# The experts' down projection in a mixture-of-experts block, taken in plain fp32 instead of high and low halves

## Chip, core and metric

The kernel runs on one core of a Trainium2 chip. The metric is the time of the whole program on the device in microseconds, the median of several runs. TensorE (PE) multiplies, VectorE (DVE) and ScalarE (ACT) work elementwise, GpSimd (POOL) works elementwise too and issues the indexed DMAs, SyncE (SP) issues the weight loads.

## What is computed

The model is a diffusion transformer of two layers on 512 latent and 256 context tokens of width 1024, all in fp32. Each layer has an attention and then a mixture of 64 experts, of which every token takes 8. The part of the reference that matters here, cut to its core:

```python
def routed_experts(xf, top_idx, top_w, w_gate, w_up, w_down):
    ...
    def body(acc, blk):
        tok, w, e = blk
        xb = x_pad[tok]
        h = jax.nn.silu(xb @ w_gate[e]) * (xb @ w_up[e])
        return acc.at[tok].add((h @ w_down[e]) * w[:, None]), None
    ...
```

A block is up to 128 tokens of one expert; xb is 128 x 1024, h is 128 x 256. The weights of one expert are 3 MB in fp32.

## The kernel before

The program is a row of stages with a barrier between them: modulation, projections, attention, output projection, routing, experts, combination, and the same again for the second layer. The change is in `stage_experts(l, nt, moe)`, which runs once per layer. Each engine has its own program there; they meet by semaphores.

All engines walk through the same steps (`all_steps`): a loop over pairs of experts, so that the buffer index j (0 or 1) is a constant, and inside it a loop over the blocks of an expert whose bounds are read from `starts_i`. Most experts have one block; where one has more, the further ones are steps without change of expert. `step(b, j, change, e, split)` is the step of block b; with `change`, block b is the first of expert e+1, and `split` says that the weights of expert e+2 are split in this step.

To reach near fp32 precision with the fast fp32r operands, every factor is kept as a high half (a copy rounded to fp32r) and a low half (the original minus the high half), and `product` forms three products for each pair: high with high, high with low, low with high. The halves:

- gate and up weights: raw in `gu_raw`, ScalarE writes `gu_hi` (L1524), VectorE `gu_lo` (L1590).
- down weights: raw in `d_raw`, ScalarE writes `d_hi` (L1530), GpSimd `d_lo` (L1404, `split_down`).
- the rows of the block, gathered into `xb` (L1395), are turned on TensorE into `psX` (L1457), and split into `xT_hi` (L1514) and `xT_lo` (L1582).
- the hidden rows `hh` (L1585: silu(gate) times up) are turned into `psH` (L1467), and split into `hT_hi` (L1553, ScalarE) and `hT_lo` (L1606, VectorE).

TensorE's order in one step is: turn the hidden rows of block b-1; the gate and up product of block b, 24 products of 512 columns into `psG`; turn the gathered rows of block b+1; the down product of block b-1, 12 products of 512 columns into `psY`. ScalarE's order: `hT_hi`, the two high halves of gate and up, silu, `xT_hi`, the left half of `yb` out of `psY`, the high half of down. VectorE's: `hT_lo`, the two low halves of gate and up, the gating product, `xT_lo`, the right half of `yb`. GpSimd's: wait for the scatter of the step before, copy its index (`si`), gather the rows of block b+2, scatter block b-1 (a DMA that adds into `acc_d`), then the low half of down.

SyncE loads the raw weights in six parts of 512 KB per expert, in the order gate, gate, up, up, down, down, with at most three parts in flight (AWAY = 3). Each raw buffer has room for two experts, and so have the halves. A raw buffer is loaded anew when its split is done: before part 0 SyncE waits for the low half of gate, before part 2 for that of up, and before part 4 for that of down:

```python
elif m == 4:
    sp.wait_ge(s_dl, e + 1)
```

The waits of the down product are:

```python
def down_of(b, j, e):
    pe.wait_ge(s_hTl, b + 1)
    pe.wait_ge(s_dl, e + 1)
    pe.wait_ge(s_ya, b + 1)
    pe.wait_ge(s_yd, b + 1)
    down(j)
```

Of the kernel before, what the change touches and what calls it, by code (L numbers as in the profile page):

```python
# [6 lines left out]
F32 = mybir.dt.float32  # L7
# [3 lines left out]
F32R = mybir.dt.float32r  # L11
ALU = mybir.AluOpType
# [3 lines left out]
P = 128  # L16
D = 1024
# [90 lines left out]
def build(nc, a, out):  # L108
    with ExitStack() as whole:
# [1192 lines left out]
        def stage_experts(l, nt, moe):  # L1302
# [6 lines left out]
            with ExitStack() as ctx:  # L1309
# [6 lines left out]
                d_hi = T("d_hi", [P, 2, KF, D], F32R)  # L1316
                d_lo = T("d_lo", [P, 2, KF, D], F32R)
# [5 lines left out]
                hT_hi = T("hT_hi", [P, KF, P], F32R)  # L1323
                hT_lo = T("hT_lo", [P, KF, P], F32R)
# [9 lines left out]
                s_guh, s_gul, s_dh, s_dl = S("guh"), S("gul"), S("dh"), S("dl")  # L1334
                s_tx, s_gu, s_ht, s_dn = S("tx"), S("gu"), S("ht"), S("dn")
                s_xh, s_xl, s_sil, s_mul, s_hTh, s_hTl, s_ya, s_yd = (S(n) for n in ("xh", "xl", "sil", "mul", "hTh", "hTl", "ya", "yd"))
# [26 lines left out]
                with nc.Block() as block:  # L1363
                    @block.sync
                    def _(sp):
                        with sp.Fori(0, NE // 2 - 1) as i:
                            for j in range(2):
                                e = 2 * i + j
                                for m in range(PARTS):

                                    if m == 0:
                                        sp.wait_ge(s_gul, 2 * e + 1)
                                    elif m == 2:
                                        sp.wait_ge(s_gul, 2 * e + 2)
                                    elif m == 4:
                                        sp.wait_ge(s_dl, e + 1)
                                    sp.sem_inc(s_bear, 1)


                                    sp.wait_ge(s_raw[m % AWAY], raw_loads(e + 2, m) - 16)  # L1380
                                    sp.sem_inc(s_bear, 1)
                                    load_part(sp, l, moe, j, e + 2, m)

                    @block.gpsimd
                    def _(pool):
# [16 lines left out]
                        def split_down(j, e):  # L1402
                            pool.wait_ge(s_dh, e + 1)
                            G.tensor_tensor(d_lo[:, j], d_raw[:, j], d_hi[:, j].bitcast(F32), ALU.subtract).then_inc(s_dl, 1)  # L1404

# [18 lines left out]
                        split_down(0, 0)  # L1424
# [4 lines left out]
                        split_down(1, 1)  # L1429

                        def step(b, j, change, e, split):
                            take_rows(b - 1)
                            pool.wait_ge(s_tx, b + 2)
                            gather(b + 2)
                            give(b - 1)
                            if split:
                                split_down(j, e + 2)
# [11 lines left out]
                    def _(pe):  # L1449
# [20 lines left out]
                        def down(j):  # L1470
                            for n in range(2):
                                c = slice(n * 512, (n + 1) * 512)
                                product(nc, psY[:, n], [(hT_hi[:, k], hT_lo[:, k], d_hi[:, j, k, c], d_lo[:, j, k, c]) for k in range(KF)], s_dn if n == 1 else None)
# [9 lines left out]
                        def down_of(b, j, e):  # L1483
                            pe.wait_ge(s_hTl, b + 1)
                            pe.wait_ge(s_dl, e + 1)
                            pe.wait_ge(s_ya, b + 1)
                            pe.wait_ge(s_yd, b + 1)
                            down(j)

                        def step(b, j, change, e, split):  # L1490
# [8 lines left out]
                            down_of(b - 1, j, e)  # L1499

                        def last(b):
                            pe.wait_ge(s_mul, b)
                            turn_hidden()
                            down_of(b - 1, 1, NE - 1)
# [6 lines left out]
                    def _(act):  # L1511
# [14 lines left out]
                        def split_down(j, e, loading=True):  # L1526
                            if loading:
                                for m in (4, 5):
                                    act.wait_ge(s_raw[m % AWAY], raw_loads(e, m))
                            nc.scalar.activation(d_hi[:, j], d_raw[:, j], ACT.Copy).then_inc(s_dh, 1)  # L1530


# [3 lines left out]
                        split_down(0, 0, False)  # L1536
# [3 lines left out]
                        split_down(1, 1, False)  # L1540
# [10 lines left out]
                        def hidden(b):  # L1551
                            act.wait_ge(s_ht, b + 1)
                            nc.scalar.activation(hT_hi[:], psH[:, 0:KF], ACT.Copy).then_inc(s_hTh, 1)  # L1553

                        def step(b, j, change, e, split):
# [9 lines left out]
                            if split:  # L1565
                                split_down(j, e + 2)
# [8 lines left out]
                    def _(dve):  # L1575
# [28 lines left out]
                        def hidden(b):  # L1604
                            dve.wait_ge(s_hTh, b + 1)
                            V.tensor_tensor(hT_lo[:], psH[:, 0:KF], hT_hi[:].bitcast(F32), ALU.subtract).then_inc(s_hTl, 1)  # L1606

                        def step(b, j, change, e, split):
                            hidden(b - 1)
# [7 lines left out]
                        def last(b):  # L1617
                            hidden(b - 1)
                            out_of(b - 1)
# [513 lines left out]
```

## Time and profile before

| | |
|---|---|
| median of 3 runs | 3462.98 us (3459.09 to 3465.24) |
| span of the profiled execution | 3452.0 us |
| PE busy | 2794.7 us (81%) |
| DVE busy | 2159.4 us (63%) |
| ACT busy | 1509.0 us (44%) |
| POOL busy | 1260.6 us (37%) |
| DMA | 643.04 MB, mean 186 GB/s |
| splits of down weights | x128 on ACT and x128 on POOL |
| blocks of both layers | 144 |

The profiled execution spans 3452.0 us from its first to its last instruction; the times of the runs also hold what lies around it, some 11 us. The two stages of the experts run from about 838 to 1830 us and from about 2490 to 3415 us. Busy times are sums over the whole program, so they do not tell which wait ends last in a stage.

### The profile page before, as it was taken

Reading aid. Unit: us, or ns where it says so; the run is one execution under the profiler, and the core shown is the slowest. Engines: PE = TensorE matmul, PEld = TensorE weight load, DVE = VectorE, ACT = ScalarE, POOL = GpSimd, SP = SyncE. Lnnn points to the kernel's source line nnn. Section 1 sums busy time; section 2 is a strip of 40 time slices with the busy share of each in tenths; the row PEclk is TensorE's granted clock in tenths of the full one; section 3 lists DMA queues with packets and bytes.
Section 4 is the critical chain, followed back from the end, with each engine's and each line's share of the span. In section 5 each row is a group of like instructions: output and inputs, shape, how many; then the busy total and the mean of one; then the engine's idle time right before and its main releaser. Section 6 shows DMA issues by size and latency. Waiting matters only on the chain. (4 is left out here: it accounts for less than half of the span.)

```text
span 3452.0 us, 46471 instructions
## 1 busy us (share of the span) xinstructions
PE 2794.7 (81%) x12826; PEld 2105.5 (61%) x12827; DVE 2159.4 (63%) x2406; ACT 1509.0 (44%) x2033; POOL 1260.6 (37%) x856
## 2 busy tenths in 40 slices
PE   8899999877888888778882788867788877888884
PEld 2266677754666676566661677756476656666663
DVE  7733345436666657878764465543667878778884
ACT  5521334312555545555552233322255655555552
POOL 1000000111555546555564000002165655556554
PEclk9999999988989999999995999988899999998997
DMA  9820100232898888999982111002489999889994
GB/s 357 316 74 5 37 1 1 71 135 107 252 275 268 252 228 260 294 289 291 287 236 88 56 38 37 19 5 113 186 245 280 273 287 285 267 270 271 278 286 133
DMA packets 206943, 643.04 MB, mean 186 GB/s; under 512 B 30664, under 2 KB 41928, under 8 KB 206336
## 3 DMA queue, kind: packets, MB, share of 16 engines
q1 hardware_dynamic: 162464, 518.83, 42.9%
q0 software_dynamic: 43232, 118.78, 16.5%
q10 hardware_dynamic: 1152, 4.19, 0.3%
q8 instruction: 57, 0.93, 0.1%
q14 instruction: 38, 0.31, 0.0%
HBM read 587.06 MB, written 90.28 MB: 196 GB/s over the span
## 5 line engine op out<-in xcount | busy, mean ns | idle before, releaser
L1590 DVE TENSOR_TENSOR F_gu_lo<-gu_raw,F_gu_hi 128x2048 fp32r<-128x2048 f32 x256 | 996.6, 3932 | 178.4 <-ACT F_gu_hi L1524 177.0
L1404 POOL TENSOR_TENSOR F_d_lo<-d_raw,F_d_hi 128x2048 fp32r<-128x2048 f32 x128 | 657.6, 5138 | 0.0
L101 PE MATMUL F_psG<-F_gu_hi,F_xT_hi 128*128 128x512 f32 x1152 | 506.7, 440 | 76.6 <-DVE F_xT_lo L1582 74.0
L102 PE MATMUL F_psG<-F_gu_lo,F_xT_hi 128*128 128x512 f32 x1152 | 488.4, 424 | 0.0
L103 PE MATMUL F_psG<-F_gu_hi,F_xT_lo 128*128 128x512 f32 x1152 | 487.6, 423 | 0.0
L1524 ACT ACTIVATE F_gu_hi<-gu_raw 128x2048 fp32r<-128x2048 f32 x256 | 475.6, 1913 | 13.3 <-PEq L126 13.3
L101 PEld LDWEIGHTS F_psG<-F_gu_hi,F_xT_hi 128*128 128x128 f32 x1152 | 241.4, 210 | 147.1 <-issue 78.6
L1457 PE MATMUL F_psX<-cst,F_xb 128*128 128x128 f32 x1168 | 173.3, 295 | 146.6 <-DMA F_xb<-f_d,F_gi 146.2
L1409 POOL COPY F_si<-tok 128x1 int32 x144 | 83.2, 578 | 552.1 <-DMA acc_d<-F_yb,F_si 552.0
L1399 POOL DMA_INDIRECT acc_d<-F_yb,F_si x146 | 232.5, 1592 | 118.5 <-issue 93.0
L103 PEld LDWEIGHTS F_psG<-F_gu_hi,F_xT_lo 128*128 128x128 f32 x1152 | 240.0, 208 | 56.8
L1549 ACT ACTIVATE F_yb<-F_psY,wgt 128x512 f32<-128x512 f32 x144 | 99.1, 688 | 399.3 <-POOL F_si L1409 299.3
L102 PEld LDWEIGHTS F_psG<-F_gu_lo,F_xT_hi 128*128 128x128 f32 x1152 | 241.6, 210 | 49.7
L1457 PEld LDWEIGHTS F_psX<-cst,F_xb 128*128 128x128 f32 x1168 | 151.9, 194 | 190.2 <-DMA F_xb<-f_d,F_gi 186.2
L1514 ACT ACTIVATE F_xT_hi<-F_psX 128x512 fp32r<-128x512 f32 x292 | 158.8, 596 | 220.0 <-PE F_psX L1457 220.0
L101 PE MATMUL F_psY<-F_d_hi,F_hT_hi 128*128 128x512 f32 x576 | 250.5, 435 | 4.6 <-DVE F_hT_lo L1606 4.6
L1530 ACT ACTIVATE F_d_hi<-d_raw 128x2048 fp32r<-128x2048 f32 x128 | 243.7, 1904 | 0.0
L103 PE MATMUL F_psY<-F_d_hi,F_hT_lo 128*128 128x512 f32 x576 | 237.9, 413 | 0.0
L102 PE MATMUL F_psY<-F_d_lo,F_hT_hi 128*128 128x512 f32 x576 | 236.8, 411 | 0.0
L1582 DVE TENSOR_TENSOR F_xT_lo<-F_psX,F_xT_hi 128x512 fp32r<-128x512 f32 x292 | 186.7, 679 | 41.8 <-ACT F_xT_hi L1514 41.8
L1395 POOL DMA_INDIRECT F_xb<-f_d,F_gi x148 | 161.2, 1089 | 128.6 <-ACT F_yb L1549 71.3
L954 POOL TENSOR_TENSOR h<-h,D_y 128x1024 f32<-128x1024 f32 x10 | 23.6, 2360 | 413.3 <-DVE D_y L937 413.3
(306 smaller groups left out, 4903.5 us busy)
## 6 DMA issues: line engine op xcount, KB each, us to landing
gu_raw<-in_we_gate_dram SPq DMA_DIRECT2D x256, 512.0 KB
gu_raw<-in_we_up_dram SPq DMA_DIRECT2D x256, 512.0 KB
d_raw<-in_we_down_dram SPq DMA_DIRECT2D x256, 512.0 KB
wada<-in_w_ada_dram SPq DMA_DIRECT2D x24, 2048.0 KB, 11.0
I_w_raw<-in_wc_in_dram SPq DMA_DIRECT2D x32, 384.0 KB, 5.8
acc_d<-o SPq DMA_DIRECT2D x12, 512.0 KB, 2.6
f_d<-D_f SPq DMA_DIRECT2D x10, 512.0 KB, 2.6
H_ac<-acc_d SPq DMA_DIRECT2D x10, 512.0 KB, 8.9
```

The costliest lines, as they stand in the source:

```text
L101: nc.tensor.matmul(acc, xh, wh, start=(start and i == 0), stop=False)
L102: nc.tensor.matmul(acc, xh, wl, start=False, stop=False)
L103: ins = nc.tensor.matmul(acc, xl, wh, start=False, stop=(stop and i == n - 1))
L1395: pool.indirect_dma_start(xb[:], None, f_d[l][0:nt * P], bass.IndirectOffsetOnAxis(ap=gi[:].bitcast(U32), axis=0), bounds_check=nt * P - 1 ...
L1399: pool.indirect_dma_start(acc_d[l], bass.IndirectOffsetOnAxis(ap=si[:].bitcast(U32), axis=0), yb[:], None, compute_op=ALU.add).then_inc(s_ ...
L1404: G.tensor_tensor(d_lo[:, j], d_raw[:, j], d_hi[:, j].bitcast(F32), ALU.subtract).then_inc(s_dl, 1)
L1457: ins = nc.tensor.transpose(psX[:, k // 4, k % 4], v[:, k], ident)
L1514: nc.scalar.activation(xT_hi[:, 4 * n:4 * n + 4], psX[:, n], ACT.Copy).then_inc(s_xh, 1)
L1524: nc.scalar.activation(gu_hi[:, j, v], gu_raw[:, j, v], ACT.Copy).then_inc(s_guh, 1)
L1530: nc.scalar.activation(d_hi[:, j], d_raw[:, j], ACT.Copy).then_inc(s_dh, 1)
L1582: V.tensor_tensor(xT_lo[:, k], psX[:, n], xT_hi[:, k].bitcast(F32), ALU.subtract).then_inc(s_xl, 1)
L1590: V.tensor_tensor(gu_lo[:, j, v], gu_raw[:, j, v], gu_hi[:, j, v].bitcast(F32), ALU.subtract).then_inc(s_gul, 1)
```

## The change

The down product takes `d_raw` itself and one `hT`, both plain fp32. The high and low halves of the down weights and of the turned hidden rows are gone, and so are the tiles that held them. Four matmul calls of 512 columns stand where twelve stood. Because TensorE now reads the raw buffer, SyncE's wait before part 4 is for a new semaphore, `s_last`, which TensorE raises after the last down product of an expert has ended; TensorE waits for its own product there. The down product now waits for the loads of the parts 4 and 5.

```diff
-                d_hi = T("d_hi", [P, 2, KF, D], F32R)
-                d_lo = T("d_lo", [P, 2, KF, D], F32R)
...
-                hT_hi = T("hT_hi", [P, KF, P], F32R)
-                hT_lo = T("hT_lo", [P, KF, P], F32R)
+                hT = T("hT", [P, KF, P])
...
                                     elif m == 4:
-                                        sp.wait_ge(s_dl, e + 1)
+                                        sp.wait_ge(s_last, e + 1)
                                     sp.sem_inc(s_bear, 1)
...
-                        def split_down(j, e):
-                            pool.wait_ge(s_dh, e + 1)
-                            G.tensor_tensor(d_lo[:, j], d_raw[:, j], d_hi[:, j].bitcast(F32), ALU.subtract).then_inc(s_dl, 1)
...
                         def down(j):
                             for n in range(2):
                                 c = slice(n * 512, (n + 1) * 512)
-                                product(nc, psY[:, n], [(hT_hi[:, k], hT_lo[:, k], d_hi[:, j, k, c], d_lo[:, j, k, c]) for k in range(KF)], s_dn if n == 1 else None)
+                                for k in range(KF):
+                                    ins = nc.tensor.matmul(psY[:, n], hT[:, k], d_raw[:, j, k, c], start=(k == 0), stop=(k == KF - 1))
+                            ins.then_inc(s_dn, 1)
...
-                        def down_of(b, j, e):
-                            pe.wait_ge(s_hTl, b + 1)
-                            pe.wait_ge(s_dl, e + 1)
+                        def down_of(b, j, e, change):
+                            pe.wait_ge(s_hT, b + 1)
+                            for m in (4, 5):
+                                pe.wait_ge(s_raw[m % AWAY], raw_loads(e, m))
                             pe.wait_ge(s_ya, b + 1)
                             pe.wait_ge(s_yd, b + 1)
                             down(j)
+                            if change:
+                                pe.wait_ge(s_dn, b + 1)
+                                pe.sem_inc(s_last, 1)
...
-                            nc.scalar.activation(d_hi[:, j], d_raw[:, j], ACT.Copy).then_inc(s_dh, 1)
...
-                            nc.scalar.activation(hT_hi[:], psH[:, 0:KF], ACT.Copy).then_inc(s_hTh, 1)
+                            nc.scalar.activation(hT[:], psH[:, 0:KF], ACT.Copy).then_inc(s_hT, 1)
...
-                            V.tensor_tensor(hT_lo[:], psH[:, 0:KF], hT_hi[:].bitcast(F32), ALU.subtract).then_inc(s_hTl, 1)
```

GpSimd in a step with a change of expert, before: index copies, gather (`F_xb`), scatter (`acc_d`), then the split of down.

```order
L1409 COPY F_si<-tok 128x1
L1433 REGISTER_ALU
L1392 ISA
L1392 COPY F_gi<-tok 128x1
L1393 REGISTER_ALU
L1395 DMA F_xb<-f_d,F_gi 128x1024
L1412 REGISTER_ALU
L1399 DMA acc_d<-F_yb,F_si 896x1024
L1403 REGISTER_ALU
L1404 TENSOR_TENSOR F_d_lo<-d_raw,F_d_hi 128x2048
L1347 TENSOR_LOAD starts_i
```

The same step after the change.

```order
L1402 COPY F_si<-tok 128x1
L1424 REGISTER_ALU
L1389 ISA
L1389 COPY F_gi<-tok 128x1
L1390 REGISTER_ALU
L1392 DMA F_xb<-f_d,F_gi 128x1024
L1405 REGISTER_ALU
L1396 DMA acc_d<-F_yb,F_si 896x1024
L1344 TENSOR_LOAD starts_i
```

The split `F_d_lo` behind the scatter is gone; the rest keeps its order. ScalarE in the same step, before, from the turned hidden rows to the end.

```order
L1553 ACTIVATE F_hT_hi<-F_psH 128x256
L1523 ISA
L1524 ACTIVATE F_gu_hi<-gu_raw 128x2048
L1523 REGISTER_ALU
L1524 ACTIVATE F_gu_hi<-gu_raw 128x2048
L1560 REGISTER_ALU
L1517 ACTIVATE F_sil<-F_psG 128x256
L1562 REGISTER_ALU
L1514 ACTIVATE F_xT_hi<-F_psX 128x512 x2
L1549 ISA
L1549 ACTIVATE F_yb<-F_psY,wgt 128x512
L1530 ACTIVATE F_d_hi<-d_raw 128x2048
```

And after.

```order
L1539 ACTIVATE F_hT<-F_psH 128x256
L1518 ISA
L1519 ACTIVATE F_gu_hi<-gu_raw 128x2048
L1518 REGISTER_ALU
L1519 ACTIVATE F_gu_hi<-gu_raw 128x2048
L1546 REGISTER_ALU
L1512 ACTIVATE F_sil<-F_psG 128x256
L1548 REGISTER_ALU
L1509 ACTIVATE F_xT_hi<-F_psX 128x512 x2
L1535 ISA
L1535 ACTIVATE F_yb<-F_psY,wgt 128x512
```

`F_d_hi` at the end is gone, and the two high halves of gate and up stand, as before, ahead of the silu, the turned rows and the output.

## Rows read from the trace of the kernel before

**Rows 1.** The page's head.

```profile
span 3452.0 us, 46471 instructions
```

**Rows 2.** Table by stretch: PE, PEld, DVE, ACT, POOL busy us; clock, DMA share, GB/s.

```profile
2700.00:3000.00 300.00, 241.05 (x1012) 187.37 (x1013) 238.25 (x155) 168.53 (x174) 174.10 (x109) 0.92 0.92 282
```

**Rows 3.** List of waits from 2500 to 3400: us in total, times, longest.

```profile
POOL F_si L1409 <- DMA acc_d<-F_yb,F_si: 257.6, 66, 6.4
```

**Rows 4.** Timeline of GpSimd in one step: start us, duration, work [idle before].

```profile
2837.29 0.74 POOL L1409 COPY F_si<-tok 128x1 int32 x1 [3.66 <-DMA acc_d<-F_yb,F_si]
...
2840.99 1.60 POOL L1399 DMA_INDIRECT acc_d<-F_yb,F_si  x1 [0.90 <-issue]
2842.03 5.18 POOL L1404 TENSOR_TENSOR F_d_lo<-d_raw,F_d_hi 128x2048 fp32r<-128x2048 f32 x1
2850.60 1.02 POOL L1409 COPY F_si<-tok 128x1 int32 x1 [3.38 <-DMA acc_d<-F_yb,F_si]
```

**Rows 5.** Timeline of GpSimd: a step without split; ends of a 25-step run.

```profile
1120.67 1.59 POOL L1399 DMA_INDIRECT acc_d<-F_yb,F_si  x1 [0.30 <-issue]
1127.06 0.18 POOL L1409 COPY F_si<-tok 128x1 int32 x1 [4.80 <-DMA acc_d<-F_yb,F_si]
...
1397.06 0.19 POOL L1409 COPY F_si<-tok 128x1 int32 x1 [4.21 <-DMA acc_d<-F_yb,F_si]
...
1741.58 0.18 POOL L1409 COPY F_si<-tok 128x1 int32 x1 [3.90 <-DMA acc_d<-F_yb,F_si]
```

**Rows 6.** List of waits of SyncE's queue, 2500 to 3400.

```profile
SPq L1377 <- POOL F_d_lo L1404: 245.4, 61, 6.8
```

**Rows 7.** Timeline of SyncE's queue: issues of weight parts, in pairs.

```profile
2840.54 2.83 SPq L1023 DMA_DIRECT2D gu_raw<-in_we_up_dram  x2
2847.44 0.92 SPq L1023 DMA_DIRECT2D d_raw<-in_we_down_dram  x2
2850.87 2.21 SPq L1023 DMA_DIRECT2D gu_raw<-in_we_gate_dram  x2
```

**Rows 8.** The page's groups: work, count | busy us, mean ns | idle before, releaser.

```profile
L1404 POOL TENSOR_TENSOR F_d_lo<-d_raw,F_d_hi 128x2048 fp32r<-128x2048 f32 x128 | 657.6, 5138 | 0.0
L1524 ACT ACTIVATE F_gu_hi<-gu_raw 128x2048 fp32r<-128x2048 f32 x256 | 475.6, 1913 | 13.3 <-PEq L126 13.3
L1409 POOL COPY F_si<-tok 128x1 int32 x144 | 83.2, 578 | 552.1 <-DMA acc_d<-F_yb,F_si 552.0
```

**Rows 9.** One line of VectorE: count, min/median/max ns, first and last start.

```profile
L1590 DVE TENSOR_TENSOR F_gu_lo<-gu_raw,F_gu_hi x256: 2276/2290/8040, 841.7 to 3387.3; 128x2048 fp32r<-128x2048 f32 x128
```

**Rows 10.** Timeline of VectorE: the gating product.

```profile
2851.50 0.41 DVE L1585 TENSOR_TENSOR F_hh<-F_sil,F_psG 128x256 f32<-128x256 f32 x1
```

**Rows 11.** Timeline of TensorE: gate_up starts, down's first and last, hidden turned, gate_up.

```profile
2839.65 0.49 PE L101 MATMUL F_psG<-F_gu_hi,F_xT_hi 128*128 128x512 f32 x1 [0.77 <-DVE F_xT_lo L1582]
...
2846.06 0.48 PE L101 MATMUL F_psY<-F_d_hi,F_hT_hi 128*128 128x512 f32 x1
...
2848.67 0.39 PE L103 MATMUL F_psY<-F_d_hi,F_hT_lo 128*128 128x512 f32 x1
2851.96 0.68 PE L1467 MATMUL F_psH<-cst,F_hh 128*128 128x128 f32 x2 [2.91 <-DVE F_hh L1585]
2853.24 0.79 PE L101 MATMUL F_psG<-F_gu_hi,F_xT_hi 128*128 128x512 f32 x1 [0.60 <-issue]
```

**Rows 12.** Timeline of TensorE: a plain fp32 down product of the shared expert.

```profile
2446.53 3.70 PE L1139 MATMUL E_psY<-E_wd,E_hT 128*128 128x512 f32 x8 [0.80 <-ACT E_hT L1195]
```

**Rows 13.** The page's DMA queues: packets, MB, share of 16 engines' span.

```profile
q1 hardware_dynamic: 162464, 518.83, 42.9%
q0 software_dynamic: 43232, 118.78, 16.5%
```

**Rows 14.** The page's DMA issues: count, size of each, median us to landing.

```profile
f_d<-D_f SPq DMA_DIRECT2D x10, 512.0 KB, 2.6
```

## What the change was predicted to do

> **What bounds the kernel now.** The change touches only the stage of the experts, so I looked at the two long stretches of that stage first. The table by stretch [rows 2] shows DMA at 0.92 of its 16 engines, TensorE busy 80% (241.05 of 300 us), VectorE 79%, and a granted clock of 0.92: no engine is full, only DMA is near it. The list of waits [rows 3] says what the rhythm hangs on: GpSimd waits 257.6 us, 66 times, of the second stage for the scatter of the step before. The GpSimd timeline [rows 4] shows the loop: copy of the index at 2837.29, scatter issued at 2840.99, landed 9.6 us later at 2850.60. 3.7 us of issue and 9.6 us of landing make a step of 13.3 us. Over a long run of steps the copy starts at 1397.06 and 25 steps later at 1741.58 [rows 5], so a steady step takes 344.5 / 25 = 13.78 us. Where a block belongs to the same expert as the one before, so that no weights are split, the scatter issued at 1120.67 has landed at 1127.06 [rows 5]: 6.4 us. The landing is long where weight loads run beside it.
>
> Second, the weight loads. SyncE waits 245.4 us, 61 times, for the split of the down weights on GpSimd [rows 6]; at 2847.44 the loads start 0.3 us after that split ends (2842.03 + 5.13 = 2847.16) [rows 4, 7]. So the stream of loads runs as far ahead as its buffers allow: a raw buffer is free as soon as the split of the weights is done, two steps before they are multiplied.
>
> **What is removed, and its worth.** Per expert: on ScalarE the high half of the down weights (128x2048 like a gate or up half, 1.91 us [rows 8]), on GpSimd the low half, 5.14 us [rows 8], per block a small low half on VectorE. GpSimd's 5.14 us lie inside the 9.6 us in which it would wait for the scatter anyway [rows 4], so without it GpSimd only waits longer: worth nothing directly. But it slows VectorE: the low halves of gate and up take 2.29 us in the median and up to 8.04 us [rows 9]. After the change I count them at 2.29 us. The Trainium skill, page SBUF — State Buffer, section "SBUF: two separate sides", says that the port pair that GpSimd and a VectorE operation with two inputs in SBUF share is an exclusive lock, so the loser waits for the whole operation; 2.29 + 5.14 = 7.4 us would be such a case, and by that rule the change is a gain for VectorE.
>
> **What is dearer: the product itself.** Now 12 products of 512 columns; the last of them starts 2848.67 - 2846.06 = 2.61 us after the first and takes 0.39: 3.0 us [rows 11]. The same product in plain fp32 (two stationary tiles, two halves of 512 columns) stands in the trace before, in the shared expert: 8 records in 3.70 us [rows 12]. So +0.7 us at full clock, and at 1.2 GHz up to twice that; I take +0.8. Where TensorE is not what ends the step this is covered by its waits, such as 2.91 us before the turn of the hidden rows [rows 11].
>
> **What is moved: the release of the buffers.** This is the term that decides. The down weights of expert x+2 can now be loaded only when down(x) has read its buffer, at the end of its step; before, it was when they had been split, two steps earlier. On SyncE's queue the four gate and up parts of expert x+3 stand behind these two. They have to be split on ScalarE in the very next step and multiplied in the one after. The queue of prefetch falls from over one step ahead to nothing, and a loop closes over two steps:
> end of down(x), six parts landed (L), second half copied on ScalarE 1.91, its low half 2.29 [rows 8, 9], from the start of the gating product to the start of gate_up 2853.24 - 2851.50 = 1.74, from the start of gate_up over the turned rows to the start of down 2846.06 - 2839.65 = 6.41 [rows 10, 11], down 3.70 [rows 12], issue on SyncE 0.33 (the second of a pair ends its issue so much after its start; an estimate from the 0.92 us of a pair [rows 7]). Without L this is 16.4 us.
> L comes from the queues [rows 13]: the hardware queue moved 518.83 MB in 42.9% of 3452 us, 2.85 us per MB, so the 3.15 MB of an expert need 8.98 us; the software queue needs 16.5% of 3452 / 118.78 = 4.8 us per MB, the scatter (0.52 MB) 2.5 us. A transfer of 512 KB alone lands 2.6 us after its issue [rows 14], 1.1 more than its 1.5 us of work. With half of the scatter inside the burst L is 11.3, with all of it 12.6. The scatter of down(x) starts with the burst, so I take 12.1. Bounds: no sharing at all, 10.1; and by the parts of now, where the second of the pair issued at 2840.54 was out by 2843.04 and let the next go at 2850.87 [rows 7], 7.8 us with three in flight, 2.6 each, 15.6 for six.
> The clock: at 0.92 granted [rows 2], some 0.16 of the time is at 1.2 GHz, half of whose work is lost: 0.08 x 13.8 = 1.1 us a step. That lies in TensorE's waits now and on the path then, with one pass of TensorE per two steps: +1.1.
> Step after: (12.1 + 16.4 + 1.1) / 2 = 14.8 us. At the bounds of L without and with the clock: 13.3 (then the scatter's 13.78 holds) and 16.6. GpSimd's own loop, 3.7 + some 11 if the scatter shares the whole burst, is about as long, so it gives no relief. In return, the gather falls into the lull behind the burst; its wait on TensorE is hidden by then.
>
> **The sum.** There are 144 blocks, 128 of them with a new expert [rows 8]; 16 are repeats. A repeat and the step behind it have their loads early, and each stage has about four steps of run-in and run-out; that leaves 144 - 32 - 8 = 104 steady steps and 40 others. Steady: 104 x (14.8 - 13.78) = +106. Others: bound by TensorE, 40 x 0.8 = +32. At the start of both stages the first splits of down go, some 2 us of ScalarE each: -4. Sum +134 on a span of 3452.0 [rows 1]: 3586. The median of the runs, 3463, is 11 us above the span, so 3597, rounded to 3600.
>
> **The rivals.**
> (a) The loads keep up (L near its lower bound, 13.3 < 13.78), the scatter sets the step as now. Then only the other steps pay: +28, 3490. For it: DMA has some 7% of lull now; against: the sum above 12 us.
> (b) Faster. GpSimd is free and VectorE's two low halves take 4.6 us, where one alone now takes up to 8.04 [rows 9]; in the step shown the gating product comes at 2851.50 and TensorE has waited 2.91 us for it [rows 10, 11]. It decides if L stays under 10.5 and if the scatter, which today meets loads in any phase, then lands against fewer of them: with 0.8 us less landing a step, 104 x -0.8 + 28 = -55, 3408. For it: the scatter that lands in 6.4 us [rows 5]. Against: the burst starts with the scatter.
> (c) Much slower. TensorE's single long wait per step lets the clock fall in most steps; with 4 us instead of 1.1 and L at 13, the step is 16.7, +304 + 28, 3795.
> (d) Gains and losses cancel within 7 us, 3463.
>
> **How the numbers follow.** Chances: the forecast 0.62, (a) 0.13, (b) 0.12, (c) 0.08, (d) 0.05. Predicted is the forecast's 3600. The range takes in (a) and (d) and steps up to 15.8 us in the forecast: 3458 to 3710; (b) and (c) are left out. A measurement of this kernel can tell about 0.2%, 7 us, from no change. Faster 0.12, within 0.2% 0.06, slower 0.82.
>
> **What would show it.** In the trace after, the list of SyncE's waits should be led by the product of down, the pair of down loads should be issued within a microsecond of its end and the gate loads right behind, ScalarE should wait for DMA before the high halves of gate and up (it does nowhere now), and TensorE longer before the turn of the hidden rows; VectorE's low halves should be at 2.3 us. A burst shorter than 10.5 us, or ScalarE not waiting for loads, would prove the forecast wrong; so would a scatter that lands in 8 us.

## The result and the profile after

The changed kernel takes 3861.18 us (3844.42 to 3863.99, 4 runs) against 3461.03 us before, a ratio of 1.1139 with an interval of 1.1112 to 1.1166: 11.4% slower, 400 us. The forecast was 3600 us, range 3458 to 3710. The direction and the mechanism held, the size did not: the loss is 400 us where some 140 were forecast.

The head and some groups of the page after, to be set beside [rows 1, 8, 9]. The columns are work, count | busy, mean ns | idle before, releaser.

```profile
span 3862.3 us, 44917 instructions
...
PE 2986.9 (77%) x12250; PEld 2071.3 (54%) x12251; DVE 1687.9 (44%) x2262; ACT 1290.6 (33%) x1905; POOL 636.4 (16%) x728
...
L1574 DVE TENSOR_TENSOR F_gu_lo<-gu_raw,F_gu_hi 128x2048 fp32r<-128x2048 f32 x256 | 585.0, 2292 | 1153.6 <-ACT F_gu_hi L1519 1153.2
L1519 ACT ACTIVATE F_gu_hi<-gu_raw 128x2048 fp32r<-128x2048 f32 x256 | 487.2, 1913 | 910.4 <-DMA gu_raw<-in_we_gate_dram 666.7
```

VectorE, ScalarE and GpSimd work less than before, TensorE more, and VectorE's low halves are at 2.29 us in the mean, 2364 ns at most, as forecast; and everything ends later. ScalarE, which waited for no load before [rows 8], is now idle for 910.4 us before its high halves, 666.7 us of it until a load of the gate weights lands. The waits of SyncE's queue over the whole program (us, times, longest), beside [rows 6]:

```profile
SPq L1374 <- PEq L1483: 1127.5, 123, 27.5
```

L1483 is TensorE's signal that down has ended. The loads wait for it once per expert, up to 27.5 us. By stretch, from 3000 to 3300, beside [rows 2]:

```profile
3000.00:3300.00 300.00, 220.34 (x755) 150.67 (x756) 118.19 (x106) 105.64 (x121) 58.08 (x71) 0.82 0.76 227
```

The DMA share fell from 0.92 to 0.76 and the granted clock from 0.92 to 0.82. How a step goes is told by the timelines of the same 35 us (start us, duration, work [idle before, releaser]). TensorE:

```profile
3113.05 3.60 PE L1463 MATMUL F_psY<-d_raw,F_hT 128*128 128x512 f32 x8
...
3126.99 3.60 PE L1463 MATMUL F_psY<-d_raw,F_hT 128*128 128x512 f32 x8
...
3136.28 0.70 PE L1456 MATMUL F_psH<-cst,F_hh 128*128 128x128 f32 x2 [5.70 <-DVE F_hh L1569]
3137.56 0.79 PE L101 MATMUL F_psG<-F_gu_hi,F_xT_hi 128*128 128x512 f32 x1 [0.58 <-DVE F_xT_lo L1566]
3138.14 0.63 PE L102 MATMUL F_psG<-F_gu_lo,F_xT_hi 128*128 128x512 f32 x1
3138.57 0.63 PE L103 MATMUL F_psG<-F_gu_hi,F_xT_lo 128*128 128x512 f32 x1
...
3143.26 0.53 PE L102 MATMUL F_psG<-F_gu_lo,F_xT_hi 128*128 128x512 f32 x1
3143.63 0.39 PE L103 MATMUL F_psG<-F_gu_hi,F_xT_lo 128*128 128x512 f32 x1
3143.86 0.40 PE L101 MATMUL F_psG<-F_gu_hi,F_xT_hi 128*128 128x512 f32 x1
...
3146.81 3.60 PE L1463 MATMUL F_psY<-d_raw,F_hT 128*128 128x512 f32 x8
```

SyncE's issues and ScalarE's high halves:

```profile
3116.97 0.90 SPq L1023 DMA_DIRECT2D d_raw<-in_we_down_dram  x2
3118.37 3.20 SPq L1023 DMA_DIRECT2D gu_raw<-in_we_gate_dram  x2
3123.13 2.66 SPq L1023 DMA_DIRECT2D gu_raw<-in_we_up_dram  x2
```

```profile
3129.21 1.91 ACT L1519 ACTIVATE F_gu_hi<-gu_raw 128x2048 fp32r<-128x2048 f32 x1 [9.62 <-DMA gu_raw<-in_we_gate_dram]
3131.66 1.91 ACT L1519 ACTIVATE F_gu_hi<-gu_raw 128x2048 fp32r<-128x2048 f32 x1 [0.54 <-DMA gu_raw<-in_we_up_dram]
```

VectorE and GpSimd:

```profile
3133.60 2.29 DVE L1574 TENSOR_TENSOR F_gu_lo<-gu_raw,F_gu_hi 128x2048 fp32r<-128x2048 f32 x1 [0.16 <-ACT F_gu_hi L1519]
3135.81 0.41 DVE L1569 TENSOR_TENSOR F_hh<-F_sil,F_psG 128x256 f32<-128x256 f32 x1
```

```profile
3115.09 1.05 POOL L1392 DMA_INDIRECT F_xb<-f_d,F_gi  x1 [0.87 <-POOL F_gi L1389]
3118.36 1.59 POOL L1396 DMA_INDIRECT acc_d<-F_yb,F_si  x1 [2.21 <-DVE F_yb L1586]
3128.64 0.19 POOL L1402 COPY F_si<-tok 128x1 int32 x1 [8.69 <-DMA acc_d<-F_yb,F_si]
```

Follow one turn of the loop. Down ends at 3113.05 + 3.60 = 3116.65. 0.3 us later the six parts begin to go out. The last part of up is there at 3131.66, 15.0 us after the end of down. Then come the high half (1.94 us until the low half starts), the low half (2.21 until the gating product at 3135.81), the turned hidden rows (1.75 until gate_up starts at 3137.56), and the next down but one at 3146.81, ended at 3150.41. 15.01 + 1.94 + 2.21 + 1.75 + 9.25 + 3.60 = 33.76 us for two steps. Between them lies a short step (3116.65 to 3130.59), which runs on loads that came in time, and a long one of 19.8 us. From the down product at 3044.69 to the one 14 steps later at 3283.45 a step takes 17.05 us, where it took 13.78 [rows 5]. Below, L is the time from the end of down to the start of the high half of the last up part.

### The profile page after: what moved, and what is told of

It reads as the page before. It is cut to its first block and busy times, and to the rows that moved or that the text cites. A ratio compares the mean times of both kernels' runs of the same rounds, so it can differ in the third digit from the quotient of the medians.

```text
span 3862.3 us, 44917 instructions
## 1 busy us (share of the span) xinstructions
PE 2986.9 (77%) x12250; PEld 2071.3 (54%) x12251; DVE 1687.9 (44%) x2262; ACT 1290.6 (33%) x1905; POOL 636.4 (16%) x728
## 5 line engine op out<-in xcount | busy, mean ns | idle before, releaser
L1574 DVE TENSOR_TENSOR F_gu_lo<-gu_raw,F_gu_hi 128x2048 fp32r<-128x2048 f32 x256 | 585.0, 2292 | 1153.6 <-ACT F_gu_hi L1519 1153.2
L1519 ACT ACTIVATE F_gu_hi<-gu_raw 128x2048 fp32r<-128x2048 f32 x256 | 487.2, 1913 | 910.4 <-DMA gu_raw<-in_we_gate_dram 666.7
L101 PE MATMUL F_psG<-F_gu_hi,F_xT_hi 128*128 128x512 f32 x1152 | 567.3, 492 | 50.7 <-DVE F_xT_lo L1566 50.7
L102 PE MATMUL F_psG<-F_gu_lo,F_xT_hi 128*128 128x512 f32 x1152 | 540.2, 469 | 0.0
L103 PE MATMUL F_psG<-F_gu_hi,F_xT_lo 128*128 128x512 f32 x1152 | 534.9, 464 | 0.0
L1463 PE MATMUL F_psY<-d_raw,F_hT 128*128 128x512 f32 x1152 | 521.8, 596 | 0.9 <-ACT F_hT L1539 0.9
L1456 PE MATMUL F_psH<-cst,F_hh 128*128 128x128 f32 x288 | 85.6, 389 | 499.4 <-DVE F_hh L1569 392.7
L1456 PEld LDWEIGHTS F_psH<-cst,F_hh 128*128 128x128 f32 x288 | 46.5, 205 | 611.5 <-DVE F_hh L1569 456.0
L1463 PEld LDWEIGHTS F_psY<-d_raw,F_hT 128*128 128x128 f32 x1152 | 209.1, 192 | 210.2 <-issue 208.8
L1586 DVE TENSOR_SCALAR F_yb<-F_psY,wgt 128x512 f32<-128x512 f32 x144 | 107.3, 745 | 87.5 <-PE F_psY L1463 78.1
L101 PE MATMUL I_psC<-I_w_hi,aT_hi 128*128 128x384 f32 (+1 forms) x384 | 127.9, 333 | 21.3 <-DVE I_w_lo L1885 12.9
```

The source lines that it names most:

```text
L101: nc.tensor.matmul(acc, xh, wh, start=(start and i == 0), stop=False)
L102: nc.tensor.matmul(acc, xh, wl, start=False, stop=False)
L103: ins = nc.tensor.matmul(acc, xl, wh, start=False, stop=(stop and i == n - 1))
L1456: ins = nc.tensor.transpose(psH[:, k], v[:, k], ident)
L1463: ins = nc.tensor.matmul(psY[:, n], hT[:, k], d_raw[:, j, k, c], start=(k == 0), stop=(k == KF - 1))
L1519: nc.scalar.activation(gu_hi[:, j, v], gu_raw[:, j, v], ACT.Copy).then_inc(s_guh, 1)
```

## The experiments

All were set against runs of the kernel before on the same chip, whose median was 3459 to 3462 us; the ratios are to these, with their interval. Differences to the changed kernel or between versions are differences of medians, mostly from different chips, and some 7 to 10 us of them can be noise. A name such as "late release" stands for one kernel.

**Late release alone.** The kernel before, all its halves kept; `pe.wait_ge(s_dn, b + 1); pe.sem_inc(s_last, 1)` after the last down product of an expert, and

```diff
-                                        sp.wait_ge(s_dl, e + 1)
+                                        sp.wait_ge(s_last, e + 1)
```

> The kernel before with all its high and low halves, and only the release moved: TensorE waits for its own down product at the end of an expert's last block and raises a semaphore, and SyncE waits for that instead of for GpSimd's split before it loads the down weights anew. Theory R (the late release, with the gate and up parts queued behind it, is the cause of the 400 us): the two-step loop closes here too, at 3.0 us of down instead of 3.6, so 3800 to 3860 us. Theory P (the plain fp32 product and the clock it leaves are the cause, the moved release is hidden): within 30 us of 3461. Theory W (TensorE's own wait, with the register loads behind it, is the cause): the same as the run with that wait alone.

3804.78 us, 1.0993 (1.0975 to 1.1012). So 343 of the 400 us come with the moved release and TensorE's own wait before its signal, with every split kept; theory P falls. SyncE's longest item is again TensorE's signal:

```profile
SPq L1378 <- PEq L1492: 1087.4, 124, 27.1
```

**TensorE's own wait alone.** The same without the change on SyncE.

> The kernel before, and only TensorE's wait for its own down product at the end of an expert's last block added (with a semaphore that nobody waits for). In the trace after, 2.0 us lie between the end of down and the turn of the hidden rows in the steps that wait for nothing else. Theory W (that wait is a good part of the loss): 124 steps x 2.0 us, up to 3700 us. Theories R and P: the 2.0 us fit into TensorE's wait of 2 to 3 us per step, so 3461 to 3500.

3465.02 us, 1.0007 (0.999 to 1.0023): no difference. The wait is really there, it is only covered; in its list of waits from 2700 to 3000 stands

```profile
PE F_psH L1468 <- issue: 36.7, 16, 2.5
```

where the kernel before has VectorE's product as the releaser of such waits [rows 11]. TensorE would wait for the hidden rows at that place anyway. Theory W falls.

**Plain product from a copy, early release.** ScalarE copies the down weights where it made their high half; SyncE waits for the copy; GpSimd's split and TensorE's own wait stay away.

```diff
-                                        sp.wait_ge(s_last, e + 1)
+                                        sp.wait_ge(s_dh, e + 1)
...
-                                    ins = nc.tensor.matmul(psY[:, n], hT[:, k], d_raw[:, j, k, c], start=(k == 0), stop=(k == KF - 1))
+                                    ins = nc.tensor.matmul(psY[:, n], hT[:, k], d_cp[:, j, k, c], start=(k == 0), stop=(k == KF - 1))
...
+                            nc.scalar.activation(d_cp[:, j], d_raw[:, j], ACT.Copy).then_inc(s_dh, 1)
```

> The changed kernel with the plain fp32 product, but from a copy: ScalarE copies the down weights of expert e+2 into a buffer of its own where it made their high half before, and SyncE waits for that copy, so the raw buffer is free as early as before; no wait of TensorE for itself. GpSimd's split stays away. Theory R: the loss goes, 3430 to 3500 us (dearer product +30, VectorE's faster low halves to its credit). Theory P: the loss stays, 3750 to 3860. Theory W: near R, as the wait is gone too; the run with the wait alone tells these apart.

3452.07 us, 0.9976 (0.9963 to 0.9989). The whole loss is gone, with the product in plain fp32. A copy that takes ScalarE 1.9 us per expert saves the 400 us. SyncE's wait for the buffer of down, 2700 to 3000, is next to nothing:

```profile
SPq L1375 <- ACT F_d_cp L1522: 3.4, 4, 1.5
```

**Gate and up ahead of down.** The changed kernel, late release and own wait kept, but on SyncE's queue the four parts of expert e+3 go before the two down parts of e+2.

```diff
-                                        sp.wait_ge(s_last, e + 1)
...
+                                gu_parts(1 - j, e + 3)
+                                d_parts(j, e + 2)
```

> The changed kernel with SyncE's queue in another order: the four gate and up parts of expert e+3 are issued before the two down parts of expert e+2, so that they no longer stand behind the wait for down(e); each part has its own semaphore, and explicit waits keep three parts in flight as before. The late release of the down buffer and TensorE's own wait stay. Theory R in its narrow form (what costs is the gate and up parts queued behind the wait, not the late loading of the down weights themselves): 3450 to 3560 us. Theory R in its wide form (the late down weights arrive too late too): above 3700. Theory P: 3800 or more.

In this version each of the six parts has a semaphore of its own, and a part still goes out only when the one three places before it has landed. 3479.81 us, 1.0056 (1.0037 to 1.0075). 381 of the 400 us are gone although the down weights are still loaded late. So the loss is not the late down weights: it is what stood behind their wait in the queue. The narrow form of theory R holds.

**Why the burst takes 15 us: the depth.** The changed kernel with `PARTS, AWAY = 6, 6`.

> The changed kernel with up to six weight parts in flight instead of three, each on its own semaphore; the order of SyncE's queue and the late release stay. In the trace after, the burst from the end of down to the last landed part of gate and up takes 15 us, not the 12.1 us of the forecast, and single parts take 4 to 8 us from issue to landing. Theory Q (three in flight are too few to fill the DMA engines while the scatter is under way): the burst falls to 12 or 13 us, the step by 1 to 1.5 us, 3700 to 3760 us. Theory C (the burst and the scatter together fill the DMA engines, so depth does not help): 3830 to 3880.

3842.71 us, 1.1105 (1.108 to 1.113): 18 us less than with three in flight (1.1139), where 100 or more were expected of theory Q; the two intervals overlap, so that even this gain isn't sure. More depth hardly shortens the burst that sets the loop. The number is that of theory C, and its reason fits too: between the first and the last two microseconds of a burst the DMA engines are nearly full, with six in flight

```profile
3066.20:3077.10 10.90, 10.90 (x41) 7.87 (x40) 0.00 (x0) 1.22 (x2) 0.97 (x1) 0.84 0.93 287
```

as with three in flight (the turn shown above):

```profile
3117.00:3119.00 2.00, 0.34 (x3) 0.34 (x3) 0.55 (x1) 0.47 (x1) 0.65 (x1) 1.00 0.63 184
3119.00:3129.60 10.60, 10.60 (x41) 7.70 (x40) 0.00 (x0) 0.77 (x2) 1.32 (x3) 0.84 0.95 286
3129.60:3131.60 2.00, 0.99 (x3) 0.16 (x1) 0.45 (x1) 1.52 (x1) 1.05 (x1) 1.00 0.49 199
```

The last but one figure is the busy share, 0.93 and 0.95, against 0.63 and 0.49 at the two ends.

**The scatter's share.** The changed kernel; of each block only 16 rows are added.

```diff
-                            pool.indirect_dma_start(acc_d[l], bass.IndirectOffsetOnAxis(ap=si[:].bitcast(U32), axis=0), yb[:], None,
+                            pool.indirect_dma_start(acc_d[l], bass.IndirectOffsetOnAxis(ap=si[0:16].bitcast(U32), axis=0), yb[0:16], None,
```

> The changed kernel, whose scatter adds only the first 16 of the 128 rows of a block, so 112 rows of each block's result are left out of the sum; every step and wait stays. It measures what the scatter takes from the burst of weight loads. By the forecast's own sum the scatter is 2.5 us of DMA work inside the burst: L 15 down to 12.5, two-step loop 33.7 down to 31.2, step 15.6, 104 x -1.25 and some of the others: 3700 to 3740 us. If the scatter costs the burst nothing: 3830 or more. If it costs more than its work (the engines slow down for it): under 3680.

3701.19 us, 1.07 (1.0671 to 1.0729): 160 us less than the change, at the lower edge of what was expected, near what the forecast's price of 2.5 us of DMA work for the whole scatter makes of it.

**The same in the kernel before.**

> The kernel before, whose scatter adds only the first 16 of the 128 rows of a block, the other 112 rows left out of the sum. If the landing of the scatter (9.6 of 13.3 us) sets the step of the kernel before, as the forecast has it, the step falls until TensorE (about 11 us with its clock) or the loads (9 us of work) or VectorE's chain with its slow low halves end it: 12 to 12.8 us, 3310 to 3400 us. If another chain of the same length (VectorE's low halves beside GpSimd's split) sets it too: 3430 or more.

3345.42 us, 0.9673 (0.965 to 0.9696), 114 us less than the 3459.77 us beside it. The landing of the scatter does set the step of the kernel before.

**The gather's share**, cut to 16 rows in the same way.

> The changed kernel, whose gather fetches only the first 16 of the 128 rows of a block, the other rows keep what they held; the scatter is whole. In the trace after, the gather is issued within a microsecond or two of the end of down, so it runs inside the burst of weight loads, where the forecast had put it into the lull behind. If so, it takes its own DMA work from the burst, 4.8 us per MB over 0.28 to 0.52 MB, 1.4 to 2.5 us of L, half of that per step: 3720 to 3790 us. If it lies in the lull: 3840 or more.

3803.54 us, 1.0978 (1.0953 to 1.1003). 58 us less, 14 us above the upper limit of the case in which the gather lies in the burst and well under the other: a part of it does lie there. But L falls by 0.4 us only (table below), half of which is 0.2 us a step or some 20 us; what gives the rest isn't shown.

**Both cut.**

> The changed kernel with gather and scatter both cut to 16 of 128 rows. Only the weight loads are then in the burst. If L is DMA work plus 1.1 us, as the forecast's lower bound has it, L falls to 10.1 us and the step to the time of TensorE and the chain behind, 13.5 us: about 3560 us. If a part of L is fixed by three parts in flight and their latency, L stays above 12 and the time above 3620.

3652.82 us, 1.0543 (1.0515 to 1.0572). One turn: its down ends at 3060.27 + 3.60 = 3063.87, and the last part is there at 3076.14:

```profile
3060.27 3.60 PE L1463 MATMUL F_psY<-d_raw,F_hT 128*128 128x512 f32 x8
```

```profile
3076.14 1.91 ACT L1519 ACTIVATE F_gu_hi<-gu_raw 128x2048 fp32r<-128x2048 f32 x1 [1.16 <-DMA gu_raw<-in_we_up_dram]
```

12.3 us with next to nothing beside the loads, where the forecast had 10.1 and 0.33 of issue for that. This turn is one of the short ones: the mean is 13.05 us (table below). The time is over the 3620 us above which the burst is slow by itself: the second case holds.

**Both cut, six in flight.**

> The changed kernel with gather and scatter cut to 16 of 128 rows, and up to six weight parts in flight. With three in flight the burst still takes 13.0 us there, where the sum of work and one lead-in gave 10.1. If the depth makes up the 3 us, L falls to 10 or 11 and the time from 3653 to 3520 to 3580. If not (the loads alone need that long in a burst, whatever the depth): 3630 to 3660.

3628.46 us, 1.0489 (1.0466 to 1.0511): 24 us less than with three in flight, 2 us below the case in which the depth does nothing and 48 above the other. One turn of it: down starts at 3024.49, ends at 3028.09, and the last part is there at 3039.99, 11.9 us after it.

```profile
3024.49 3.60 PE L1463 MATMUL F_psY<-d_raw,F_hT 128*128 128x512 f32 x8
```

```profile
3039.99 1.92 ACT L1519 ACTIVATE F_gu_hi<-gu_raw 128x2048 fp32r<-128x2048 f32 x1 [0.59 <-DMA gu_raw<-in_we_up_dram]
```

Between these two turns the depth gives 0.4 us, and 0.45 between the means of 13.05 and 12.6 us: a small part of what L has too much.

**Idle products against the low clock.** The changed kernel, with this after the signal:

```diff
+                                for _ in range(4):
+                                    nc.tensor.matmul(psW[:], ident, cst[:, 0:512], start=True, stop=True)
```

> The changed kernel with four idle fp32 products of 512 columns on constants after the last down product of an expert (into a bank that nobody reads), so that TensorE works in the first 3.6 us of its long wait. In the trace after, gate_up after the wait takes 8.3 us instead of 5.7, as the clock is at 1.2 GHz for its first part, where the forecast had charged 1.1 us per two steps. If the lower clock is a true part of the loss: granted clock up from 0.82 to 0.9 in the stage, 3740 to 3810 us. If the loads alone set the pace: 3850 to 3900, since the idle products delay the short step.

3820.72 us, 1.105 (1.1015 to 1.1085). Its stretch from 3000 to 3300, with 0.90 granted where the change had 0.82:

```profile
3000.00:3300.00 300.00, 267.65 (x885) 167.69 (x884) 121.97 (x111) 108.76 (x128) 58.14 (x70) 0.90 0.75 220
```

The clock rose as expected, the time fell by 40 us and not by 50 to 120, 11 us short of what was expected. But this doesn't price the low clock. The stretch is at a higher mean clock because the idle products and the short steps are; the products behind the long wait, on which the loop hangs, are still at the lower clock there:

```profile
3099.97 3.67 PE L1486 MATMUL F_psW<-cst 128*128 128x512 f32 x8
3105.82 0.70 PE L1457 MATMUL F_psH<-cst,F_hh 128*128 128x128 f32 x2 [2.17 <-DVE F_hh L1572]
3107.09 0.79 PE L101 MATMUL F_psG<-F_gu_hi,F_xT_hi 128*128 128x512 f32 x1 [0.58 <-DVE F_xT_lo L1569]
...
3116.10 3.60 PE L1464 MATMUL F_psY<-d_raw,F_hT 128*128 128x512 f32 x8
...
3123.51 0.47 PE L101 MATMUL F_psG<-F_gu_hi,F_xT_hi 128*128 128x512 f32 x1
...
3129.96 3.60 PE L1464 MATMUL F_psY<-d_raw,F_hT 128*128 128x512 f32 x8
```

From the start of gate_up to the start of down it is 3116.10 - 3107.09 = 9.0 us in the long step, hardly less than the 9.25 of the turn above without idle products, and 3129.96 - 3123.51 = 6.45 us in the short step, where it was 3126.99 - 3118.92 = 8.07 us and where it bears on nothing, as the step behind it waits for loads anyway. In the mean of the turns whose time the loads set, this part falls from 8.6 to 8.2 us only (table below). So the clock is a part of the loss, and 40 us are what these idle products give, not what the low clock takes.

**GpSimd's split away, nothing else.** The kernel before with the low halves of the first two experts used throughout.

> The kernel before, where GpSimd forms the low half of the down weights for the first two experts only, and the twelve products go on using those; so the low halves of all other experts are left out of the result. The buffers are released by ScalarE's high half. It is the removal of GpSimd's split and of its hold on VectorE alone, without the plain fp32 product; against the version with the copy it prices that product. The forecast: removal worth nothing, 3450 to 3465, and the version with the copy, 3452, then means that the product costs next to nothing where TensorE does not end the step. The other reading: the removal is worth 50 us or more, below 3410, and the dearer product eats nearly all of it in the version with the copy.

3471.15 us, 1.0032 (1.0018 to 1.0046), 6 us over what was expected. VectorE's low halves are at 2.29 us there too,

```profile
L1590 DVE TENSOR_TENSOR F_gu_lo<-gu_raw,F_gu_hi 128x2048 fp32r<-128x2048 f32 x256 | 575.2, 2289 | 178.9 <-ACT F_gu_hi L1524 177.5
L1410 POOL COPY F_si<-tok 128x1 int32 x144 | 28.7, 199 | 1165.3 <-DMA acc_d<-F_yb,F_si 1163.9
```

and GpSimd waits for its scatter 1165 us instead of 552 [rows 8]. The removal of 658 us of GpSimd's work gains nothing, it even costs 0.3%; why it costs is open. The version with the copy is 0.6% below this one, so the plain product, with the split of the hidden rows gone, is no loss in it.

**Depth where the loads are early.** First two parts in flight in the version with the copy (`PARTS, AWAY = 6, 2`):

> The version with the copy of the down weights and the plain fp32 product, but with two weight parts in flight instead of three. There the scatter of a step takes 10 us to land beside the loads, and the loads are over one step ahead. If fewer loads in flight let the scatter land sooner and the loads still keep up: 3380 to 3440 us. If two in flight are too few for 3 MB per step beside gather and scatter (a pair of parts takes some 5 us, three pairs 15 us): the loads fall behind, 3500 to 3700.

3703.14 us, 1.0696 (1.0664 to 1.0727), 3 us above the second case: the depth matters. Then six:

> The version with the copied down weights, with up to six parts in flight instead of three. The DMA engines are 0.94 busy there, and two in flight cost 240 us. If three is also still a little short: 3410 to 3440 us. If three suffice, the loads only press more on the scatter: 3452 to 3490 us.

3383.67 us, 0.9775 (0.9756 to 0.9794), better than forecast and better than both kernels. The kernel before with six:

> The kernel before with up to six weight parts in flight instead of three, nothing else. The version with the copy gained 68 us by that. If that gain belongs to the depth alone: 3380 to 3400 here. If it needs the freed engines (VectorE's low halves at 2.3 us, GpSimd without split): 3430 or more here, and only the two together gain.

3427.51 us, 0.9906 (0.9889 to 0.9924). The depth alone gives 31 us in the kernel before (against 3458.96 us beside it) and 68 us in the version with the copy, so about half of it comes only with the copied version. That lies between the two cases expected; which of the differences of that version it needs wasn't tried. In the version with the copy and six in flight the DMA engines carry 292 GB/s and TensorE's granted clock is 0.96, where the kernel before had 282 GB/s and 0.92 [rows 2]:

```profile
2700.00:3000.00 300.00, 254.59 (x979) 171.54 (x980) 155.58 (x141) 172.52 (x183) 69.33 (x92) 0.96 0.93 292
```

## Why the prediction was right in kind and wrong in size

**What bounds the kernel: right.** The landing of the scatter sets the step (its cut in the kernel before gives 114 us), GpSimd's split is covered (its removal alone gives a ratio of 1.0032), and VectorE's low halves fall to 2.29 us without gain. One reading is off by a little: the split in [rows 4] takes 5.18 us and ends at 2847.21, 0.2 us before the loads start; nothing hangs on it.

**The product, +0.8 us: nearly right.** 3.60 us against 3.0 [rows 11]. Late release alone and the change differ by 56 us. An estimate accounts for them: in a loop over two steps, with one product on it, 0.6 us are 0.3 a step, 104 x 0.3 = 31 us, and up to 0.6 in each of the 40 others, 24 us. The turns in the table below agree: 34.0 us with the plain product, 33.3 without. With an early release it costs nothing that can be seen.

**The loop over two steps: right in every link.** The release moved by two steps, gate and up queued behind it, and ScalarE waiting for them were all there, and late release alone gives 343 us. The step that failed is the size of two of its terms: L, the time of the burst of loads, and the low clock between gate_up and down. The forecast had 29.6 us for the two steps, the turn shown took 33.76, and the result lies above even rival (c), 3795. A turn here is the time from the end of one down to the end of the next but one. One turn alone may be an exception, so the table gives means over both stages, of all turns in which gate_up starts less than 6 us after the start of the last high half, so that the loads set the time:

| kernel | turns | L, us | gate_up to down, us | whole turn, us |
|---|---|---|---|---|
| forecast, with 0.33 of issue in L | | 12.4 | 7.5 | 29.6 |
| the change | 75 | 15.9 | 8.6 | 34.0 |
| late release alone | 65 | 15.9 | 8.6 | 33.3 |
| the change, six in flight | 58 | 15.3 | 8.9 | 33.65 |
| idle products | 62 | 15.55 | 8.2 | 33.2 |
| gather cut | 80 | 15.5 | 8.6 | 33.5 |
| scatter cut | 86 | 13.9 | 8.3 | 31.6 |
| both cut | 66 | 13.05 | 8.2 | 30.75 |
| both cut, six in flight | 67 | 12.6 | 8.4 | 30.5 |

- L: forecast 12.4 with the issue, measured 15.0 in the turn shown and 15.9 in the mean: +3.4. The sum took work at 2.85 us per MB from the queue's average over the whole program, half to all of the scatter, one lead-in of 1.1 us, and no gather. The gather was put "into the lull behind the burst"; it is issued at 3115.09, 1.6 us before down ends, and runs with the burst, at a price of 0.4 us of L (0.8 where the scatter is cut too). The scatter's price is 2.0 us, as taken in the sum. The rest lies with the loads: they alone need 13.05 us in the mean and not 10.4, and the depth of three is not the reason (six in flight: 0.45 us less). In the burst of the turn shown the DMA engines are busy 0.84 of 14.6 us, that is 12.3 us of work and 2.3 idle, where the forecast had 11.0 and 1.1; with both cut it is 0.81 of 11.9 us, 9.6 of work and 2.3 idle.

```profile
3117.00:3131.60 14.60, 11.92 (x42) 8.20 (x42) 0.99 (x2) 2.77 (x3) 3.02 (x4) 0.88 0.84 260
```

```profile
3064.20:3066.20 2.00, 0.00 (x0) 0.00 (x0) 0.77 (x1) 2.00 (x4) 0.00 (x0) 1.00 0.49 137
...
3074.20:3076.20 2.00, 2.00 (x10) 1.67 (x9) 1.19 (x1) 0.84 (x2) 0.00 (x0) 1.00 0.56 191
3064.20:3076.10 11.90, 7.22 (x25) 5.71 (x26) 5.57 (x6) 5.33 (x7) 1.32 (x1) 0.86 0.81 270
```

  Most of the idle time lies in the first two microseconds (0.49 busy with both cut) and the last two (0.56). The upper bound of 15.6, read from the parts' own landing times in the trace before, was the true value (15.9 less 0.33 of issue); I set it aside for a sum of averages.
- From gate_up to down, forecast 6.41 and 1.1 for the clock, measured 9.25 in the turn shown and 8.6 in the mean: +1.1. After 5.70 us of waiting the products start at the lower of the two clocks, 1.2 GHz: 3138.57 - 3138.14 = 0.43 us each, and this holds up to 3143.26, where later ones are 0.23 us apart; some 13 products at 0.20 more are 2.6 us. I charged the average share of the low clock before; the change itself made the wait longer and the clock lower. That was rival (c) in a weaker form, and it acts together with L. No run here takes the low clock off the loop: the idle products gave back 0.4 to 0.5 us of a turn, and left the long step shown with them at 9.0 us. By the table it costs 8.6 - 6.4 = 2.2 us a turn, an estimate.
- The other links together: -0.1.

Half of 34.0 - 29.6 = 4.4 us over 104 steps is +229 us on top of the forecast's +106, together 335, near the 104 x 3.27 = 340 us that the steady steps show. **The 40 other steps**, forecast +32, hold the rest: 410 us of span less 340 are 70, 1.8 us each; what they hold was not looked into. That TensorE's own wait, some 2 us, is bare there is a guess: in the kernel before it cost nothing (1.0007), and the only hint is that the order with gate and up ahead, which keeps it, is 28 us slower than the copy, which has none. It wasn't tried.

**The rivals.** (a), (b) and (d) fell by the result, and late release alone shows why. (b)'s premise, that freed engines shorten the step, was tested and found empty at three in flight; with six in flight the version with the copy is 44 us below the kernel before (3384 against 3428). One of the forecast's own signs of being wrong was badly chosen: a scatter that lands in 8 us. In the turn shown one scatter takes 3128.64 - 3118.36 = 10.3 us and the next, behind the long wait, 8.0; the median over both stages is 9.5 us against 10.1 in the kernel before. The loop closed all the same.

**The rule of the exclusive port pair**, from the Trainium skill, page SBUF — State Buffer, section "SBUF: two separate sides": the trace agrees in kind. Without GpSimd's split the 256 low halves take 2281 ns at least, 2290 in the median and 2296 at most,

```profile
L1590 DVE TENSOR_TENSOR F_gu_lo<-gu_raw,F_gu_hi x256: 2281/2290/2296, 844.0 to 3401.3; 128x2048 fp32r<-128x2048 f32 x128
```

where [rows 9] had up to 8040. In the step of [rows 4] the low half starts 0.8 us after the split does and ends 2.2 us after the split has ended, as if it had stood still for the rest of the split (2842.83 + 6.55 = 2849.38 against 2842.03 + 5.18 = 2847.21):

```profile
2842.83 6.55 DVE L1590 TENSOR_TENSOR F_gu_lo<-gu_raw,F_gu_hi 128x2048 fp32r<-128x2048 f32 x1 [1.39 <-ACT F_gu_hi L1524]
```

The longest of all, 8.04 us, is 0.6 us above the 7.4 us that the rule makes of one whole split. The gain that it promised to VectorE came, and bore on nothing that ended a step.

**What stays open.** Why the DMA engines are idle for some 2.3 us of a burst, where one lead-in was put at 1.1, and why the loads alone are 9.6 us of work in it and 9.0 by the average. Neither scatter, gather nor the depth explains it. And what the low clock on the loop is worth, for no run took it off.

## What to carry to other kernels

When a split or copy is removed because its consumer can read the raw buffer, look at who frees that buffer now, and what is queued behind that wait: a cheap copy on an engine that has time to spare can be the thing that keeps a prefetch ahead. If the release must be late, put the loads that are needed sooner in front of it; here that alone brought back 381 of 400 us. Price a burst by the landing times of the same transfers in the trace, not by the average rate of a queue. And when a run is to price the low clock, look at the steps on the path: here the mean clock of the stretch rose from 0.82 to 0.90 while the step that sets the loop stayed slow.

## What was not expected of the hardware

Two, three and six parts of 512 KB in flight gave 3703, 3452 and 3384 us in the version with the copy (the profiled run of the last is its fastest, 3369 us). From 2700 to 3000 the DMA engines were busy 0.81, 0.94 and 0.93 and moved 238, 289 and 292 GB/s; from 1450 to 1750 it was 0.79, 0.94 and 0.94 with 236, 291 and 301. A share of 0.94 doesn't tell all: with six in flight the same share moved 3% more. And taking 658 us of GpSimd's work and, with it, 421 us of VectorE's time in the low halves (996.6 to 575.2 us) out of the kernel before made it 0.3% slower, with GpSimd's wait for the scatter up from 552 to 1164 us.
